# The state space stage of a two-block kernel, rebuilt: raw input turned as it lands, z's weight slots between the pieces of the scan

## The reference, cut to what matters

```python
proj = h @ w_in
u, z = proj[..., :1024], proj[..., 1024:]
ug = u.reshape(1, 256, 64, 16)              # 64 groups of 16 channels
dt = exp(log_dt); mag = exp(lr * dt)
ab = mag * cos(li * dt), mag * sin(li * dt)  # 64 states per group, complex
f = (ab - 1) / (lr + i li)
in_ = f * einsum('blgc,gpc->blgp', ug, b)    # complex
s = associative_scan(s[t] = ab * s[t-1] + in_[t])
y = real(einsum('blgp,gcp->blgc', s, c)) + d_skip * u
y = gelu(y)
y = y * sigmoid(y @ w_glu + b_glu)
y = y * silu(z)
x = x + y @ w_out
```

## Time and profile before

| what | us |
|---|---|
| three runs | 1455.03, 1456.99, 1459.4 |
| median | 1456.99 |
| the profiled execution | 1455.84 |
| its span, first to last instruction | 1454.0 |
| PE busy in the span | 1283.2 (88%) |
| DVE busy | 964.9 (66%) |
| ACT busy | 627.1 (43%) |
| GpSimd (POOL) busy | 181.4 (12%) |
| mean granted TensorE clock | 0.946 of full |

### The profile page before, as it was taken

How to read it: one execution, slowest core, us unless ns; L and a number is a source line. 1 busy time by engine, 2 the same in 40 slices (tenths; PEclk the granted TensorE clock), 3 DMA queues, 4 the chain that set the end, 5 groups by cost and what they waited for, 6 DMA issues and landing times.

```text
span 1454.0 us, 18974 instructions
## 1 busy us (share of the span) xinstructions
PE 1283.2 (88%) x7276; PEld 1074.3 (74%) x7276; DVE 964.9 (66%) x1467; ACT 627.1 (43%) x951; POOL 181.4 (12%) x185
## 2 busy tenths in 40 slices
PE   4946379899888999999979999799999989799997
PEld 2435267678777788877779998587788877699986
DVE  4569966585655799768655665447798586565553
ACT  2123134455545455445444444344655453444442
POOL 1995500120010001010010000200010010100000
PEclk9968599999989999999989999899999999899999
DMA  6612045455254544525546656554445435455662
GB/s 214 191 58 63 18 150 171 118 180 166 73 166 127 174 159 146 174 78 183 159 134 187 187 175 198 147 165 160 145 135 170 131 125 168 135 181 183 190 191 88
DMA packets 71852, 216.81 MB, mean 149 GB/s; under 512 B 16545, under 2 KB 20017, under 8 KB 71505
## 3 DMA queue, kind: packets, MB, share of 16 engines
q1 hardware_dynamic: 68112, 205.39, 45.2%
q0 software_dynamic: 2480, 9.06, 2.1%
q10 hardware_dynamic: 1168, 1.14, 0.2%
HBM read 210.05 MB, written 3.15 MB: 147 GB/s over the span
## 4 chain that ended last, share of the span: by engine, by line
PE 77%; DVE 14%; ACT 3%; POOL 3%; issue 2%; DMA 1%; ACTq 0%; SPq 0%; POOLq 0%; DVEq 0%
PE acc L580 16%; PE acc L581 16%; PE acc L582 16%; PE acc L549 6%; PE acc L551 6%; PE acc L550 6%; PE acc L512 4%; POOL stat L1913 2%; PE turned L623 2%; DVE b_mats L1294 2%; PE mixed L769 1%; DVE scan_work L1294 1%; DVE weights_lo L1261 1%; PE mixed L779 1%; DVE junk L1294 1%
## 5 line engine op out<-in xcount | busy, mean ns | idle before, releaser
L1261 DVE TENSOR_TENSOR weights_lo<-weights_raw,weights_hi 128x1024 fp32r<-128x1024 f32 (+2 forms) x364 | 444.0, 1232 | 253.5 <-ACT weights_hi L945 252.2
L945 ACT ACTIVATE weights_hi<-weights_raw 128x1024 fp32r<-128x1024 f32 (+2 forms) x364 | 377.8, 1049 | 313.8 <-PE acc L582 198.9
L580 PE MATMUL acc<-weights_hi,act_F_hi 128*128 128x512 f32 (+1 forms) x864 | 354.8, 411 | 6.2 <-DVE weights_lo L1261 3.3
L581 PE MATMUL acc<-weights_lo,act_F_hi 128*128 128x512 f32 (+1 forms) x864 | 344.8, 399 | 0.0
L582 PE MATMUL acc<-weights_hi,act_F_lo 128*128 128x512 f32 (+1 forms) x864 | 343.9, 398 | 0.0
L549 PE MATMUL acc<-act_F_hi,weights_hi 128*128 128x256 f32 x704 | 199.5, 283 | 0.0
L550 PE MATMUL acc<-act_F_hi,weights_lo 128*128 128x256 f32 x704 | 199.0, 283 | 0.0
L551 PE MATMUL acc<-act_F_lo,weights_hi 128*128 128x256 f32 x704 | 198.9, 283 | 0.0
L580 PEld LDWEIGHTS acc<-weights_hi,act_F_hi 128*128 128x128 f32 x864 | 166.3, 192 | 43.3 <-DVE weights_lo L1261 4.4
L582 PEld LDWEIGHTS acc<-weights_hi,act_F_lo 128*128 128x128 f32 x864 | 166.2, 192 | 38.1
L581 PEld LDWEIGHTS acc<-weights_lo,act_F_hi 128*128 128x128 f32 x864 | 166.6, 193 | 35.0
(11 more groups left out here) (278 smaller groups left out, 1502.6 us busy)
## 6 DMA issues: line engine op xcount, KB each, us to landing
weights_raw<-stream_dram SPq DMA_DIRECT2D x364, 512.0 KB, 4.1
gains<-rows_dram POOLq DMA_DIRECT2D x14, 512.0 KB, 4.1
weights_raw<-stream_dram SPq DMA_DIRECT2D x8, 416.0 KB, 3.2
weights_raw<-stream_dram SPq DMA_DIRECT2D x4, 384.0 KB, 4.8
x_T<-x_in_dram SPq DMA_DIRECT2D x1, 1024.0 KB, 4.9
ssm_bc<-ssm_bc_dram POOLq DMA_DIRECT2D x1, 1024.0 KB, 5.1
u_scratch<-u_T ACTq DMA_DIRECT2D x4, 256.0 KB, 4.7
u_sub<-u_scratch SPq DMA_DIRECT2D x16, 64.0 KB, 2.7
```

The lines of the kernel that those rows point to most:

```text
L580: pe.matmul(o, xh, wh, start=first and kk == 0, stop=False)
L581: pe.matmul(o, xh, wl, start=False, stop=False)
L945: act.activation(w_hi[:, s % R, 0:n], raw[:, s % R, 0:n], ACT.Copy).then_inc(hi_made, 1)
L1261: dve.tensor_tensor(w_lo[:, s % R, 0:n], raw[:, s % R, 0:n], w_hi[:, s % R, 0:n].bitcast(F32), ALU.subtract).then_inc(lo_made, 1)
```

## The change

**Start.** x comes in four pieces between the first weight slots; PE turns raw x (`x_T`) as each piece lands, ACT copies it with the norm's gain as scale per partition (`gained`; the gain and d_skip rows are turned to columns by PE once), and the root of each row is applied as a scale when u and z leave PSUM. No normed rows are written for this norm.

**Tables.** Only the scan's 32 angles are reduced at the start; the rope tables' angles and sines are made later, behind the GLU (`rope_angles`, `rope_tables`). f is multiplied into the reversed powers, not into b. ACT rewrites the b and c tables by pair (`bcq`, channel innermost). GpSimd doubles `turns` only up to 16 of 32; DVE makes the last doubling (`last_turns`).

**Scan.** `c_mats` move to DVE as four products without sums (PE adds them: `states_part` has four products per pair), into `c_alt` and `c_mats` by turns; `c_alt`, `hn_F` and `bcq` lie in the memory of the weight halves. d * u is added as a matmul of the identity with a pattern of d to the taps. GELU works on y in PSUM: ACT squares, DVE sums, ACT tanh, DVE multiplies into `y_sub`, which is stored in one transfer and read back in two as the finished GELU. The slots of z (8 to 15) are run between the pieces of the scan; both z chunks use the first pair of PSUM banks, and the state terms the second bank of the second pair.

```diff
-            turn("hn", DT, tiles_of(hT), lambda t, k: (rows_normed, t + 1), True)
-            run(12)
+            turn("hn", DT, tiles_of(xT), lambda t, k: (x_in4[k // 2], 16), True)
+            run(4)
...
+                pe.wait_ge(d_pattern_made, 1)
+                for n in range(2):
+                    a = n * P + (SUB - 1) * GROUP
+                    i = pe.matmul(b[:, a:a + GROUP], ident, d_pat[:, 2 * qd + n, :], start=False, stop=True, skip_group_check=True)
...
+            taps(0)
+            run(1)
+            turned_taps_and_b(0)
             state_terms(0)
+            run(1)
+            taps(1)
+            run(1)
+            turned_taps_and_b(1)
+            own_steps(0)
+            states_part(0)
+            state_terms(1)
+            run(3)
+            taps(2)
+            run(1)
+            turned_taps_and_b(2)
+            state_terms(2)
+            own_steps(1)
+            states_part(1)
+            run(1)
+            taps(3)
+            turned_taps_and_b(3)
+            state_terms(3)
+            own_steps(2)
+            states_part(2)
+            own_steps(3)
+            states_part(3)
...
+            ssm_steps = {8: lambda: (load_u(0), load_u(1)), 12: lambda: load_u(2), 13: lambda: toeplitz(0), 15: lambda: toeplitz(1),
+                         16: lambda: load_u(3), 18: lambda: y_to_rows(0), 19: lambda: toeplitz(2),
+                         20: lambda: (y_to_rows(1), toeplitz(3), y_to_rows(2), y_to_rows(3))}
...
+            act.wait_ge(dt_in, 32)
             act.activation(pdt[:, :], pdt[:, :], ACT.Exp).then_inc(dt_exp, 1)
...
+            def gelu_square(qd):
+                if qd > 0:
+                    act.wait_ge(gelu_made, qd)
+                for e in range(2):
+                    act.wait_ge(y_ready, 2 * qd + e + 1)
+                    x = act.activation(gel[:, e, :], turned_bank[e][:, 0:2 * P], ACT.Square, scale=math.sqrt(0.044715))
+                x.then_inc(y_squared, 1)
...
+            pair_c(0)
+            order_u(0)
+            run(4)
+            taps(0)
+            turned_taps_and_b(0)
+            pair_c(1)
+            group_u(0)
+            order_u(1)
...
+            act.wait_ge(y_ready, 2 * (PARTS - 1))
+            splits(WHOLE + R - 1)
+            gelu_square(3)
+            gelu_tanh(3)
...
+                tt(o[0], pr, cr, ALU.mult).then_inc(dve_steps, count())
+                tt(o[1], pi, ci, ALU.mult).then_inc(dve_steps, count())
+                tt(o[2], pr, ci, ALU.mult).then_inc(dve_steps, count())
+                dve.wait_ge(dve_steps, count.n)
+                tt(o[3], mi, cr, ALU.mult).then_inc(c_mats_made, 1)
...
-                fr, fi = (bc[:, c, :, q0:q0 + PQ].rearrange("p c q -> p q c").unsqueeze(2).broadcast_to([P, PQ, SUB, GROUP]) for c in range(2))
+                br, bi = (bcq[:, c, q0:q0 + PQ, :].unsqueeze(2).broadcast_to([P, PQ, SUB, GROUP]) for c in range(2))
...
+            def gelu_product(qd):
+                dve.wait_ge(gelu_tanh_made, qd + 1)
                 if qd > 0:
+                    dve.wait_ge(y_stored, 16 * qd)
...
             b_mats(0)
+            c_mats(0)
             b_mats(1)
+            last_turns()
+            scan_states(0)
+            c_mats(1)
+            gelu_sum(0)
+            evac("ssm_in.2")
+            b_mats(2)
+            gelu_product(0)
+            scan_states(1)
+            c_mats(2)
+            gelu_sum(1)
+            b_mats(3)
+            gelu_product(1)
+            scan_states(2)
+            c_mats(3)
+            gelu_sum(2)
+            evac("ssm_in.3")
+            gelu_product(2)
+            scan_states(3)
+            pos = WHOLE
+            dve.wait_ge(slot_used, WHOLE)
+            dve.wait_ge(c_paired, 2 * PARTS)
+            splits(WHOLE + 2)
+            gelu_sum(3)
+            gelu_product(3)
...
             turn_lo("yg", f_hi, f_lo, DT, 0.125)
-            run(8)
+            rope_angles()
+            run(4)
+            rope_tables()
+            run(4)
...
-            while n < NSUB:
+            while 2 * n < NSUB:
```

More of the change, by code:

```diff
@@ L171, in build @@
         raw = sb("weights_raw", [P, R, SLOT])
+        with ExitStack() as s0:
+            c_alt = sb("c_mats_alt", [P, 4, PQ, SUB * GROUP], F32, s0)
+            f0 = sb("hn_F", [P, DT, SEQ], F32, s0)
+            bcq = sb("ssm_by_pair", [P, 4, Q, GROUP], F32, s0)
         w_hi = sb("weights_hi", [P, R, SLOT], F32R)
@@ L668, in taps_and_turned_b @@
                 for n in range(1, 4):
[L669 to L670 removed]
+                    turned_b(qd, n)
             def state_terms(qd):
@@ L708, in states_part @@
                 pe.wait_ge(c_mats_made, qd + 1)
+                cm = (c_alt, c_mat)[qd % 2]
                 for q in range(PQ):
-                    for c in range(2):
+                    for n in range(4):
                         for e in range(2):
@@ L1069, in _, with gained @@
-            run(16)
+            def gained(k):
+                n = turn_at[f"hn.{k // 2}"][0]
+                act.wait_ge(turned, n + 1)
+                for kk in range(2):
+                    x = act.activation(f0[:, k + kk, :], turned_bank[n % 2][:, kk * SEQ:(kk + 1) * SEQ], ACT.Copy,
+                                       scale=cols_F[:, k + kk:k + kk + 1])
+                x.then_inc(turned_hi, 1)
+            act.wait_ge(cols_copied, 1)
+            gained(0)
+            gained(2)
+            act.wait_ge(angles, 1)
@@ new lines, in _ @@
+            act.activation(par[:, 3:5, :].rearrange("p a q -> p (a q)"), ang_w[:, 2 * Q:4 * Q], ACT.Sin).then_inc(sines, 1)
+            gained(4)
+            for k in range(DT // 2):
+                act.wait_ge(x_in4[k], 16)
+            a = stats_of("hn", 6)
+            for t in range(TT):
+                squares(xT[:, t, :], a[:, t:t + 1], norm_sums, t + 1)
+            gained(6)
+            act.wait_ge(ssm_mats_in, 16)
+            for n in range(4):
+                x = act.activation(bcq[:, n, :, :], bc[:, n, :, :].rearrange("p c q -> p q c"), ACT.Copy, scale=-1.0 if n == 3 else 1.0)
+                if n % 2:
+                    x.then_inc(pairs_ordered, 1)
@@ L1142, in _ @@
+            gelu_tanh(3)
+            turn_hi("y", f_hi, DT, 0.5)
             run(8)
             turn_hi("yg", f_hi, DT, 0.125)
-            run(8)
+            run(4)
+            act.wait_ge(angles, 2)
+            n = RDK + ROPE
+            flat = scan_w[:, :, :, :].rearrange("p a q k -> p (a q k)")
+            act.activation(flat[:, 2 * n:4 * n], flat[:, 2 * n:4 * n], ACT.Sin).then_inc(sines, 1)
+            run(4)
             square_sums("h1", x_updated, 3)
@@ L1431, in _ @@
-            last.then_inc(angles, 1)
+            dve.wait_ge(cols_turned, 1)
+            dve.tensor_copy(cols_F[:, :], mixed_bank[0][:, 0:2 * DT]).then_inc(cols_copied, 1)
+            reduced(ang_w[:, 0:Q], ang_w[:, Q:2 * Q], ang_w[:, 2 * Q:3 * Q], ang_w[:, 3 * Q:4 * Q])
+            dve.tensor_reduce(one_of[:, :], ident.rearrange("p (a c) -> p c a", c=GROUP), mybir.AxisListType.X, ALU.add).then_inc(dve_steps, count())
+            dve.wait_ge(cols_copied, 1)
+            dve.wait_ge(dve_steps, count.n)
```

555 lines of the change are left out of this document (279 added, 276 removed).

## The result

The changed kernel takes 1414.87 us (median of 4 runs, 1412.43 to 1417.41) against 1457.38 of the kernel before on the same occasion: ratio 0.9709, 95% interval 0.9685 to 0.9733, about 42 us faster. The forecast was 1414. Timed once more on another occasion it took 1409.2 against 1456.06: ratio 0.9678 (0.9664 to 0.9691). What differs there is told at the last experiment.

What follows compares the result with a forecast made beforehand. DVE, slowed by GpSimd, was taken to set the state space stage while PE waits. From 1455.84 us, 44 less at the first GLU slot plus 1 for rope gave 1412.8; the median adds 1.15: 1414, range 1400 to 1438.

Steps and rivals of the forecast that it cites:

- What bounded the kernel: State space stage, 78.3 to 204.07 us: DVE, slowed by GpSimd, sets the pace; PE waits, with no projection slots to fill gaps.
- Start: Ahead of the scan: turning raw x lets slot 0 start at 10.0 us and u's slots end at 37.5, where they ended at 49.5.
- The gate I named: Ahead of slot 0: the log-dt table, landing 6.7 us after issue at 8.0, then Exp, small operations and copies until 10.0.
- The scan: From u's last slot to the GLU: a path through the engine queues from 37.5 to 155.9 us.
- its surcharge: In the scan: 4 us added for about 40 hand-offs between engines, putting the first GLU slot at 160.
- Beside the path: Transfers and tables off the path: y's store 2.12 us to land, its loads 3.00, turn table in time, rope tables mostly hidden.
- The 1 us for the rope tables: Rope angles moved to DVE under the output projection: 5 us of work, mostly hidden, taken as 1 us, ends 0 and 5.
- Products stay slow: Rival in b_mats and c_mats: the repeated first input keeps products at 1.98 us each, total 1420; chance 0.15.
- Turn table late: Rival: GpSimd's turn table takes 45 us instead of 29.4, first scan 11 to 13 us later, total 1426; chance 0.1.
- Clock in the scan: Rival: PE's clock is 0.75 over the scan's small matmuls, path 17 us longer less 4.6 already counted, total 1427; chance 0.1.
- slower than before: Rival: z's slots also run below full clock; at 0.6 of full speed the path grows about 60 us, total 1474; chance 0.03.
- The order does not do what it says: Rival in the scan's queues: slots land late or a store blocks, half the gain is lost, total 1436; chance 0.07.

Runs made afterwards that it cites:

- the last experiment: The changed kernel timed once more without any edit, on another occasion, against the kernel before: 1409.2 us.
- Experiments 3: The changed kernel with c_mats, in the new layout with four products, back on GpSimd: 1424.49 us, ratio 0.9778 to the kernel before.
- 7: The kernel before with only c_mats moved from GpSimd to DVE, in the old layout of three operations a pair: 1439.16 us, ratio 0.9871.
- experiment 2: The changed kernel with b_mats alone reading the b table in its old order, in steps of 128 B: 1418.86 us, ratio 0.9755.
- experiment 4: The changed kernel with z's eight slots run in one block ahead of the scan, as before the change: 1428.75 us, ratio 0.9806.
- Experiment 5: The changed kernel with slot 0 run after the second turn of x: 1408.15 us; a second kernel also issuing x ahead of all weights: 1408.8 us.
- e7_last_slot: The changed kernel with DVE's order moved (1400.31 us), plus z's last slot behind the third part's states and its evacuation behind the third GELU: 1409.88 us.

## Why the prediction was right, step by step

**What bounded the kernel.** Right. Experiments 3 and 7 show GpSimd's company from both sides, 2 shows the step, 4 the empty gaps of PE. At the GLU slot they are worth 15.9, 16.6, 7.7 and 20.6 us, and the start 7.7. (I had the u slots of the kernel before end at 49.5; its 15 further slots start at 26.47, so the eighth ended at 50.6, and the start gained 50.6 to 42.9.) Experiments 3 and 7 are two measures of one thing; with 7, the sum is 52.6 against the 42.8 gained: the parts overlap, and the four products a pair give 3.5 us a part back on PE (5.98 against 2.48).

**Start: 5.4 us too early.** The sum said slot 0 at 10.0 and the last u slot done at 37.5; it was 12.57 and 42.89. The gate I named was the wrong one: the Exp that waits for the log-dt table ran at 4.44, since the table landed sooner than the 6.7 us taken from the earlier trace rows, and x's pieces came last, the third turned at 11.69, before slot 0 in PE's order. Experiment 5 confirms it: with slot 0 ahead of that turn, it starts at 10.25. This is 2.6 of the 5.4 us. The second miss is a term that I did not have: slot 0 took 5.92 us, and the next 3.60. That is 2.3 us, and the fourth turn behind it 0.4. It could be read before: there slot 0 started at 22.03 and the next slot at 26.47, 4.44 us for one slot and a turn, where I took 3.44.

**The scan: right without its surcharge.** I had 37.5 to 155.9, so 118.4 us, and 4 for hand-offs. Measured from 42.89 to 161.26 are 118.4. Between, the ends of the state terms of part 0, the states of part 0, of 1 and of 2 were forecast at 12.5, 31.0, 69.3 and 95.6 us behind the first taps and came at 11.9, 31.4, 67.8 and 95.3. Inside, the states were undersized (5.0, measured 5.98 each: 128 matmuls of 46.7 ns, where the row of 2.48 has 64 of 38.8), and the copies of `c_pairs` oversized (1.03 us, not 1.48). The hand-offs I had partly counted in the idle times of the copies. So the mechanism was right, but the hit within 1 us is luck: it rests on two misses of opposite sign, +5.4 at the start and -4.1 here, and the second timing, 1409.2, lies 4.8 us below the forecast. In its trace the same two misses are +3.7 and -2.2.

**Beside the path.** DVE idle at `z_T` was forecast at 6.6 us and came at 6.37. PE's busy share from the first taps to the GLU slot is 95.56 / 118.37 = 81% (over 75% forecast), the clock 0.94 there and 0.84 in the end. y's store landed in 2.3 us and its loads in 2.4. The 1 us for the rope tables would be the difference of 42.8 at the GLU slot and 42.2 in the span, 0.6 us; in these two traces 1.2 GHz holds for nearly the same time of the rest (86.0 and 86.6 us), but with 5 us of scatter between executions one pair shows no more than that the term is small.

**The rivals.** *Products stay slow*: refuted, 1.22 us with a first input that repeats its element. The Trainium skill, "Vector Engine (DVE) Microarchitecture Reference", Measured stream behaviour on trn2, read strictly, gave 1.85 (an estimate); the measurement decides: for a source that hops at each element it is near (1.97 in experiment 2), and a repeated element is not such a source. Its price was too low: slow `b_mats` alone cost 7.7 us at the GLU slot, where I had 6 for both. *Turn table late*: GpSimd worked on it for 28 us, to 45.5, and DVE asked for it at 57.8. *Clock in the scan* and *slower than before*: 1.00 until 119 us with z's slots between the pieces, where experiment 4, without them, has 0.78. With 0.88 from the first taps to the GLU slot, in the last experiment, the scan was 1.9 us longer than with 0.94. The price of the first was summed wrongly: 0.75 over the 62 us of small matmuls that the next rival names adds 20.7 us, not 17. *The order does not do what it says*: it does here, but experiment e7_last_slot shows the mechanism at its full price: one slot moved, SyncE's list not moved with it, and 9 us lost.

## What to carry to other kernels

When a stage is bound by an engine that another one slows, look first for what fills its idle time and PE's: independent weight slots between the pieces of a scan were the largest single part here, half of it through the clock. Moving work onto the busiest engine can pay when the mover's company cost as much as the work, and when part of it falls in a wait. Whenever a slot is moved, list what stands behind its release in every queue, the transfer queue too.

## What the runs showed of the hardware

- A 128x1024 float32 product on DVE with one input repeating each element takes 1.22 us, and 1.97 when the other input steps 128 B. Beside GpSimd the contiguous one takes 3.04, and operations of the scan from SBUF suffered more in the kernel before (two of 128x256 took 4.91 us, against 0.76).
- The first weight slot on PE took 4.53 to 6.12 us over the twelve traced executions that begin in this way, later ones 3.60, while the clock's column shows 1.00 for the stretch. In the changed kernel's trace its matmuls start 0.85 us apart until 16.83 us and 0.43 apart from 17.46 on: half the rate at first, as at 1.2 GHz. The trace's record of the granted clock has its first entry at 17.2 us, so the 1.00 before it is no measurement. In all fourteen traces of this case the half rate ends at the first entry.
- The same program, started on two occasions, differed by 5.0 us over the 1250 us behind the first GLU slot: 4.7 of them are PE's, with 86.6 and 74.7 us at 1.2 GHz. The mean clock of the whole execution was 0.964 in both. Gains below that need runs of both kernels on one chip, and milestones of the trace beside them; compare the clock stretch by stretch.
